# Attention stream with sorted products: the suffix sums move to even slots, and VectorE reads them behind the slot's maximum

## The reference

```python
def stick_breaking_attention(q, k, v):
    # A[t,s] = sigmoid(z_ts) * prod_{s<j<t} (1 - sigmoid(z_tj)), s < t
    z = jnp.einsum('bthd,bhsd->bhts', qb, kh) * scale
    past = s_pos[None, :] < t_pos[:, None]
    log_1m = jnp.where(past, jax.nn.log_sigmoid(-z), 0.0)
    tail = lax.cumsum(log_1m, axis=3, reverse=True) - log_1m      # the suffix sums
    w = jnp.where(past, jnp.exp(jax.nn.log_sigmoid(z) + tail), 0.0)
    return jnp.einsum('bhts,bhsd->bthd', w, vh)
```

## Time and profile before

| | |
|---|---|
| median of three runs | 3553.5 us (3552.3 to 3555.4) |
| profiled execution, its own time | 3550.7 us |
| its span | 3549.1 us |
| mean granted clock of TensorE | 0.991 |
| TensorE busy | 3452.3 us (97%) |
| VectorE busy | 1951.3 us (55%) |
| ScalarE busy | 1470.1 us (41%) |
| the two attention streams | about 261 us each |

### The profile page before, as it was taken

The page is one execution under the profiler, slowest core; times in us unless marked ns, Lnnn a source line. Parts: engine busy times, 40 slices in busy tenths (PEclk is TensorE's granted clock), DMA queues, the critical chain, the costliest instruction groups (busy, mean ns, idle before and its releaser), DMA issues.

```text
span 3549.1 us, 46490 instructions
## 1 busy us (share of the span) xinstructions
PE 3452.3 (97%) x16740; PEld 2770.3 (78%) x16740; DVE 1951.3 (55%) x3217; ACT 1470.1 (41%) x2210; POOL 174.6 (5%) x181
## 2 busy tenths in 40 slices
PE   9999999999999999999998899999999999999997
PEld 7888886667888888888866687888888777878886
DVE  5443465767544344434647765444368886545433
ACT  5432355554444234423455644443232434434431
POOL 0000000000100000000000001000100001020001
PEclk9999999999999999999999999999999999999999
DMA  4223422114322222234321043323422223313231
GB/s 142 95 100 107 157 98 72 42 39 165 139 96 99 102 98 98 95 107 142 116 81 51 28 158 139 100 98 104 141 95 95 77 78 106 118 60 106 95 107 65
DMA packets 99831, 356.06 MB, mean 100 GB/s; under 512 B 11823, under 2 KB 12079, under 8 KB 98920
## 3 DMA queue, kind: packets, MB, share of 16 engines
q1 hardware_dynamic: 83232, 300.16, 25.1%
q10 hardware_dynamic: 9416, 30.34, 2.6%
q0 software_dynamic: 7040, 23.66, 1.8%
HBM read 330.98 MB, written 26.80 MB: 101 GB/s over the span
## 4 chain that ended last, share of the span: by engine, by line
PE 86%; DVE 8%; ACT 3%; issue 3%; POOLq 0%; DMA 0%; POOL 0%; ACTq 0%; DVEq 0%; SPq 0%
PE bank L329 24%; PE bank L331 24%; PE bank L330 24%; PE bank L622 4%; PE bank L1106 1%; DVE unit_lo L308 1%; PE bank L1077 1%; PE bank L1730 1%; PE bank L1183 1%; ACT unit_hi L303 1%; PE bank L1086 1%; DVE val L1911 1%; DVE sq L1446 1%; DVE picked L1453 1%; PE bank L1746 1%
## 5 line engine op out<-in xcount | busy, mean ns | idle before, releaser
L308 DVE TENSOR_TENSOR unit_lo<-unit_raw,unit_hi 128x1024 fp32r<-128x1024 f32 x526 | 647.2, 1232 | 676.2 <-ACT unit_hi L303 665.8
L329 PE MATMUL bank<-h_hi,unit_hi 128*128 128x512 f32 x2416 | 954.3, 395 | 5.7 <-DVE h_lo L413 4.1
L331 PE MATMUL bank<-h_hi,unit_lo 128*128 128x512 f32 x2416 | 942.7, 390 | 0.0
L330 PE MATMUL bank<-h_lo,unit_hi 128*128 128x512 f32 x2416 | 942.5, 390 | 0.0
L303 ACT ACTIVATE unit_hi<-unit_raw 128x1024 fp32r<-128x1024 f32 x526 | 552.3, 1052 | 351.2 <-PE bank L331 337.8
L329 PEld LDWEIGHTS bank<-h_hi,unit_hi 128*128 128x128 f32 x2416 | 454.9, 188 | 117.0 <-issue 23.2
L331 PEld LDWEIGHTS bank<-h_hi,unit_lo 128*128 128x128 f32 x2416 | 454.7, 188 | 95.6
L330 PEld LDWEIGHTS bank<-h_lo,unit_hi 128*128 128x128 f32 x2416 | 455.0, 188 | 93.4 <-issue 1.7
L329 PE MATMUL bank<-act_hi,unit_hi 128*128 128x512 f32 x880 | 342.3, 389 | 0.0
L330 PE MATMUL bank<-act_lo,unit_hi 128*128 128x512 f32 x880 | 342.3, 389 | 0.0
L331 PE MATMUL bank<-act_hi,unit_lo 128*128 128x512 f32 x880 | 342.3, 389 | 0.0
(11 more groups left out here) (325 smaller groups left out, 4511.3 us busy)
## 6 DMA issues: line engine op xcount, KB each, us to landing
unit_raw<-in_units SPq DMA_DIRECT2D x564, 512.0 KB, 3.3
gates_kept<-gate_z POOLq DMA_DIRECT2D x32, 256.0 KB, 2.3
sig_ab<-gates_kept ACTq DMA_DIRECT2D x16, 512.0 KB, 3.6
bias_rows<-bias_once POOLq DMA_DIRECT2D x2, 3840.0 KB, 18.9
x_kept<-x ACTq DMA_DIRECT2D x3, 2048.0 KB, 11.0
x<-x_kept ACTq DMA_DIRECT2D x3, 2048.0 KB, 9.2
xc<-xc ACTq DMA_DIRECT2D x16, 256.0 KB, 4.4
bias_t<-bias_rows POOLq DMA_DIRECT2D x16, 256.0 KB, 3.8
```

The lines of the kernel that those rows point to most:

```text
L308: nc.vector.tensor_tensor(w_lo[u % SLOTS][:], raw[u % SLOTS][:], w_hi[u % SLOTS][:].bitcast(F32), ALU.subtract).then_inc(unit_lo, 1)
L329: nc.tensor.matmul(out_ap, w_h, r_h, start=first, stop=False)
L330: nc.tensor.matmul(out_ap, w_h, r_l, start=False, stop=False)
L331: return nc.tensor.matmul(out_ap, w_l, r_h, start=False, stop=last)
```

## The change

Two things. The slots in which the suffix sums are made become 12, 14 and 16, and those in which they are subtracted 13, 15 and 17. And VectorE's subtraction moves from `stick`, the last call of its slot, to `stick_z`, renamed `stick_first`, which is called right behind `reduce`. The instructions stay the same, and so do `GATE_FILL` and all other slots, the exponential's slot 17 among them.

```diff
-    Z_MADE, Z_READ, SUM_MADE, SUM_READ = (2, 4, 6), (2, 4, 6), (11, 13, 15), (12, 14, 16)
+    Z_MADE, Z_READ, SUM_MADE, SUM_READ = (2, 4, 6), (2, 4, 6), (12, 14, 16), (13, 15, 17)
...
-        def stick_z(h, slot):
+        def stick_first(h, slot):
...
                 ins.then_inc(s["sb_zm"], 1)
+            if slot in SUM_READ:
+                i = SUM_READ.index(slot)
+                dve.wait_ge(s["sb_c"], 3 * h + i + 1)
+                at, n = 512 * i, 512 if i < 2 else 256
+                nc.vector.tensor_tensor(sb_z[:, at:at + n], sb_z[:, at:at + n], bank[6][:, 0:n], ALU.subtract).then_inc(s["sb_d"], 1)
...
         def stick(h, slot):
...
-            if slot in SUM_READ:
-                i = SUM_READ.index(slot)
-                dve.wait_ge(s["sb_c"], 3 * h + i + 1)
-                at, n = 512 * i, 512 if i < 2 else 256
-                nc.vector.tensor_tensor(sb_z[:, at:at + n], sb_z[:, at:at + n], bank[6][:, 0:n], ALU.subtract).then_inc(s["sb_d"], 1)
...
             if b < TB:
-                stick_z(b, at)
+                stick_first(b, at)
```

## The result

The changed kernel takes 3520.8 us (median of four runs, 3519.7 to 3521.2) against 3552.9 us for the kernel before: a ratio of 0.9908, with a 95% interval of 0.9891 to 0.9926. It is 32 us faster by the medians. The forecast was 3525 us; the sum behind it was 27.2 us. Only fast executions are compared in what follows; of the ten of the kernel with only the new place on VectorE, one was slow, at 8858.9 us.

A forecast was written before the change was run, and what follows sets the result against it. TensorE, busy for 97% of the span, was taken as the bound; gains of 11.0, 7.9, 3.4 and 4.9 us summed to 27.2 us, giving 3525 us, between 3523.5 and 3526.3, with a range of 3515 to 3543 us.

The forecast's parts named there:

- The first sum's slot: First suffix sum, slot 11 to 12: 25.3 us of `sb_lo` waits give way to 14.3 us; gain 11.0 us.
- The clock: Five slow TensorE stretches behind first-sum waits: 7.9 us regained, bounds 0 and 10.2, half of block 3's loss kept.
- The reading under the term: TensorE behind first-sum waits: low clock follows a wait of about 3 us or more; 2.56 us cost none.
- The rival that the clock is not given back: TensorE's slow stretches stay, so only the other gains remain: 19.3 us, 3534 us; chance 0.20.
- The waits for `gate_z`: First gate product after slot 12, blocks 0 and 2: the moved first sum hides ScalarE's bank 7 copy; gain 3.4 us.
- The subtraction: VectorE's subtraction directly behind the slot's maximum: TensorE's 4.9 us of `sb_z` waits go; block 2 walked 1.9 us early.
- The first: VectorE and ScalarE don't keep up, so TensorE's wait only changes its place: 3543 us; chance 0.12.
- The slower one: VectorE, held in odd slots by late sums, delays TensorE through index sums and the next `reduce`: 3577 us; chance 0.04.

The follow-up runs named there:

- the last kernel: Changed kernel with the low part `sb_lo` made directly behind job 11's maximum, not ahead of that job's reduction: 3515.4 us, ratio 0.9884; again 3515.6 us, 0.9889.

## Why the prediction was right

**The first sum's slot.** Predicted were new waits of 1.31, 1.50, 1.91 and 2.44 us; measured 1.40, 1.48, 1.92 and 2.46 in the first layer and within 0.02 of these in the second, 14.5 us against 14.3. The step held: a wait of 25.3 us is replaced by one for the instruction that is next in VectorE's queue. The gain is 10.8 us, 11.0 were predicted.

**The clock.** Predicted 7.9 us with bounds of 0 and 10.2; measured 10.8 by TensorE's busy time, above the upper bound. The mechanism held, but this is the mis-sized term. The low stretch at 724 us of the kernel before is missing in the changed one. It stands behind no first sum and was in no term of the sum:

```profile
724.00:728.00 4.00, 4.00 (x13) 2.96 (x12) 3.90 (x12) 0.91 (x3) 0.00 (x0) 0.57 0.00 0
```

That is 1.7 us. No experiment ties it to the change, so here the forecast was helped by luck. Block 3's low stretches were halved, from 3.4 to 1.7 us in each layer by the sum of (1 - granted clock), as the term had assumed. The other microsecond is not placed. Adding up (1 - granted clock) over the two streams and what lies between gives 18.7 us before and 6.8 us after, 11.9 less; but before, about 2 us of that fell into the waits themselves, where TensorE has no work to slow down, and weighted with the busy time it is 9.7 less. So the term's size is known to a microsecond or so only.

The reading under the term was too simple. It said that low clock follows a wait of about 3 us or more. But block 1's wait in the second layer, 3.06 us, was followed by 1.00 in the kernel before, and block 3's 2.46 us in the changed kernel were followed by 1.2 GHz. Taking half of block 3's loss was a guess between these.

The rival that the clock is not given back falls, and with it, for this kernel, the application of the Trainium skill's rule ("TensorE: Matmul & The Clock Gate", section "A second HAM failure mode: psum-queue depth-cycling"): L1077 and L1183 still wait 14 times (17 before), only shorter, and the clock stayed up behind six of the eight waits of slot 12.

**The waits for `gate_z`.** Predicted 3.4 us, measured 3.9. The 0.23 us behind unit 5, which I had left out, went too. The experiment with the sums ahead of the gate products brought back exactly these six.

**The subtraction.** Predicted 4.9 us, measured 4.9, but part of the working was wrong and the size came out by luck. The prediction put all 4.9 us down to the second sum, in slot 13. That is where block 3 waits (1.37 us per layer). Block 2's 1.08 us stand at the third sum, in slot 15, as the rows above show, and its second sum, the one that was walked, did not wait for `sb_z` at all. In block 2 the subtraction was walked to be 1.9 us early. The timeline of the changed kernel gives 1.4 us, and only 0.35 us at the third sum:

```profile
682.17 0.69 DVE L1365 TENSOR_TENSOR sb_z<-sb_z,bank 128x512 f32<-128x512 f32 x1
684.26 0.42 PE L1183 MATMUL bank<-prob_r,tri_r 128*128 128x384 f32 x1
688.81 0.69 DVE L1365 TENSOR_TENSOR sb_z<-sb_z,bank 128x512 f32<-128x512 f32 x1
689.85 0.39 PE L1183 MATMUL bank<-cmp_r,tri_r 128*128 128x256 f32 x1
```

With the new slots but the subtraction at the end of its slot, the third sum waits 1.23 us; the place behind the maximum is what keeps it in time, by little. The prediction gave this part to both halves together without telling them apart.

**What it missed.** A turn in block 3 of the first layer (L1086) waits 1.31 us for ScalarE's exponential where it waited 0.21 us before, 1.1 us. The second layer of the kernel before has this wait in full:

```profile
739.20 0.66 PE L1086 MATMUL bank<-constants,prob 128*128 128x128 f32 x4 [0.21 <-ACT prob L1271]
2004.45 0.66 PE L1086 MATMUL bank<-constants,prob 128*128 128x128 f32 x4 [1.31 <-ACT prob L1271]
```

The first row stands 11 us behind the low stretch at 724 us, which had made TensorE late. In the second execution of the last kernel a low stretch (712 to 716 us) stands as far ahead of this turn, and there the wait is 0.15 us. So the longer wait is not the price of the new order; it goes with the missing low stretch, and takes back 1.1 of its 1.7 us. Another 0.4 us are new waits of L1077 outside slot 12. The waits add up to 10.8 + 3.9 + 4.9 - 1.1 - 0.4 = 18.1 us, and with 10.8 us of busy time and 0.9 us not placed that is the 29.8 us of the two spans. The four terms are thus 10.8, 10.8, 3.9 and 4.9 us against 11.0, 7.9, 3.4 and 4.9.

**The other rivals.** The first needed waits in slots 14 to 18 or at L1189: in slots 14 to 18 none has come, and L1189's 1.9 us are the old ones. The slower one needed VectorE's standstill in odd slots to reach TensorE. VectorE waits 2.9 us in all for the sums, and no line of TensorE waits for the work queued behind them.

## What to carry to other kernels

When an engine waits in the middle of its queue, put what it waits for behind work that does not need it, and then ask at once which instruction of the other engine is next in line: here the gain was the old wait minus the one for the reduction queued behind `sb_lo`, and moving that reduction forward gave another 7 us. Count a long TensorE wait at its length plus a slower clock that may follow it. Here the 10.8 us taken off the first sums' waits came with 10.8 us of busy time. But give that second part a wide range: the same wait was followed by full clock in one execution and by half clock in another. And look up in the rows which instruction a wait stands before, not only its line: the three pieces of the suffix sums share L1183, and the piece that was walked was not the one that waited.

## What the runs showed of the hardware

The clock behind a wait is not a function of the wait's length alone. In the kernel before, block 1's wait in the second layer, 3.06 us, was followed by 1.00. With the same 3.05 us in the kernel with only the new place, this is the row of the first sum; a 128x512 product that takes 0.50 us at full clock took 0.79:

```profile
1890.51 0.79 PE L1183 MATMUL bank<-prob_r,tri_r 128*128 128x512 f32 x1 [3.05 <-DVE sb_lo L1377]
```

A wait of 2.46 us was followed by low clock (block 3, changed kernel, both layers), and 2.45 us at the same place in the kernel with the sums ahead of the gate products was not, in either layer. Behind block 0's 2.55 us the clock stayed up in the kernel before, in both layers, and fell in the second layer of the kernel with only the new place. Even 1.92 us can: block 2's wait was followed by 1.00 in both executions of the changed kernel, but not in the kernel with the sums ahead of the gate products. There the clock fell 0.6 us (second layer) to 1.3 us (first) behind the wait's end; the wait of 0.86 us for `gate_z` comes 3 us and more behind it, too late to have begun the fall. These are the stretches from slot 12's scores of block 2 on, in both layers:

```profile
679.20:685.20 6.00, 5.14 (x20) 3.92 (x21) 5.02 (x14) 1.86 (x5) 0.54 (x1) 0.60 0.08 32
1935.90:1941.90 6.00, 5.13 (x22) 3.90 (x22) 5.06 (x14) 1.90 (x5) 0.54 (x1) 0.72 0.00 0
```

Behind slot 12's waits of 1.4 and 1.5 us (blocks 0 and 1) no low clock was seen in any of these kernels. But short waits are not safe: in both executions of the changed kernel a stretch of low clock (533 to 537 us) begins 1.5 to 1.7 us behind a wait of 1.3 us at the stream's start, and in one of the slots alone it followed 1.23 us.

Low clock also came with no wait near it. In the kernel with only the new place TensorE was busy for 12.94 of 13 us and then for all of the next 8, in which the clock fell:

```profile
1962.00:1975.00 13.00, 12.94 (x84) 7.47 (x83) 11.32 (x27) 7.24 (x16) 1.31 (x2) 1.00 0.16 62
1975.00:1983.00 8.00, 8.00 (x31) 4.81 (x30) 5.39 (x14) 5.41 (x11) 0.00 (x0) 0.57 0.00 1
```

So the waits explain the five low stretches that were gone once they were filled, and not every one. Of two executions of the last kernel, with nearly the same waits, one shows no low clock at all between 526 and 2060 us, and the other three low stretches, 5.1 us by the sum of (1 - granted clock). Of differences of 2 to 5 us between two profiles of such a kernel this alone can be the cause.
